# In the last three weight pieces of the mixing and dense stages, token tile 0 meets all three before tile 1 meets any

## The reference

```python
for layer in range(DEPTH):
    shift, scale, gate = ada_modulation(c, w_mod_mix[layer], b_mod_mix[layer])
    h = normalize(x) * (1.0 + scale) + shift
    mix = token_mixer(h, ...)          # projections, three branches, sigmoid gates, merged @ w_out
    x = layer_norm(DEEPNORM_ALPHA * x + (1.0 + gate) * mix, ln_mix_g[layer], ln_mix_b[layer])
    shift, scale, gate = ada_modulation(c, w_mod_ffn[layer], b_mod_ffn[layer])
    h = normalize(x) * (1.0 + scale) + shift
    ff = swiglu(h, ...) if layer % 2 == 0 else moe_swiglu(h, ...)   # dense 2816, or top 2 of 8 experts of 3584
    x = layer_norm(DEEPNORM_ALPHA * x + (1.0 + gate) * ff, ln_ffn_g[layer], ln_ffn_b[layer])
```

## Time and profile before

| | |
|---|---|
| median of 3 runs | 1868.97 us (1868.19 to 1871.65) |
| the profiled execution | 1872.58 us |
| its span in the trace | 1870.8 us |
| TensorE busy | 1721.1 us (92%) |
| VectorE busy | 1422.7 us (76%) |
| ScalarE busy | 1043.2 us (56%) |
| moved by DMA | 502.33 MB, 269 GB/s in the mean |

### The profile page before, as it was taken

One profiled execution on the slowest core, in us unless ns is written; L12 is line 12 of the kernel. 1 busy time (PEld: TensorE's weight loads), 2 busy tenths in 40 slices (PEclk: granted clock), 3 DMA queues, 4 the chain that ended last, 5 costly groups with the idle time before them and its releaser, 6 DMA issues.

```text
span 1870.8 us, 21981 instructions
## 1 busy us (share of the span) xinstructions
PE 1721.1 (92%) x7882; PEld 1380.4 (74%) x7883; DVE 1422.7 (76%) x1201; ACT 1043.2 (56%) x817; POOL 25.6 (1%) x31
## 2 busy tenths in 40 slices
PE   1899979997999958998999989999999999999995
PEld 0787758886877737876878878888788787787884
DVE  7776877766776785886888875556588788888887
ACT  1465434433455335765767755545477676776773
POOL 0100000000100000000000000000000000000000
PEclk9898989999999978999999999999999999999998
DMA  9874458765674345996998975676599899899991
GB/s 364 314 272 157 156 181 305 279 225 180 230 244 158 116 177 179 364 361 251 365 354 310 367 279 176 210 230 214 178 369 370 291 369 369 291 367 343 340 365 69
DMA packets 210536, 502.33 MB, mean 269 GB/s; under 512 B 9137, under 2 KB 13409, under 8 KB 210481
## 3 DMA queue, kind: packets, MB, share of 16 engines
q1 hardware_dynamic: 208770, 496.15, 74.7%
q0 software_dynamic: 1712, 5.43, 1.0%
HBM read 500.50 MB, written 1.05 MB: 268 GB/s over the span
## 4 chain that ended last, share of the span: by engine, by line
PE 84%; DVE 10%; issue 3%; ACT 1%; DMA 1%; POOL 0%; DVEq 0%; SPq 0%; ACTq 0%; POOLq 0%
PE ps L1343 24%; PE ps L1344 23%; PE ps L1345 23%; PE ps L1349 2%; PE ps L1350 2%; PE ps L1737 2%; PE ps L1850 2%; DVE mod_acc L853 1%; DVE w_lo L828 1%; PE ps L1778 1%; DVE stats L873 1%; PE ps L1467 1%; DVE gates L1022 1%; DVE hbuf L904 1%; DVE hbuf L907 1%
## 5 line engine op out<-in xcount | busy, mean ns | idle before, releaser
L1224 DVE TENSOR_TENSOR w_lo<-w_raw,w_hi 128x2048 fp32r<-128x2048 f32 x333 | 762.3, 2291 | 227.6 <-ACT w_hi L716 219.8
L716 ACT CAST w_hi<-w_raw 128x2048 fp32r<-128x2048 f32 x333 | 635.7, 1911 | 245.3 <-PE ps L1345 181.1
L1343 PE MATMUL ps<-w_hi,actT_hi 128*128 128x512 f32 (+1 forms) x1536 | 609.6, 397 | 22.5 <-issue 12.6
L1345 PE MATMUL ps<-w_hi,actT_lo 128*128 128x512 f32 (+1 forms) x1536 | 596.6, 388 | 0.0
L1344 PE MATMUL ps<-w_lo,actT_hi 128*128 128x512 f32 (+1 forms) x1536 | 596.2, 388 | 0.0
L1343 PEld LDWEIGHTS ps<-w_hi,actT_hi 128*128 128x128 f32 x1536 | 291.7, 190 | 88.2 <-issue 27.7
L1345 PEld LDWEIGHTS ps<-w_hi,actT_lo 128*128 128x128 f32 x1536 | 291.2, 190 | 60.5
L1344 PEld LDWEIGHTS ps<-w_lo,actT_hi 128*128 128x128 f32 x1536 | 292.0, 190 | 58.5 <-issue 2.4
L828 DVE TENSOR_TENSOR w_lo<-w_raw,w_hi 128x2048 fp32r<-128x2048 f32 x90 | 205.9, 2290 | 117.8 <-ACT w_hi L464 117.6
L464 ACT CAST w_hi<-w_raw 128x2048 fp32r<-128x2048 f32 x90 | 171.4, 1909 | 128.8 <-PE ps L1345 120.1
L1343 PE MATMUL ps<-w_hi,gT_hi 128*128 128x512 f32 x536 | 218.0, 407 | 17.0 <-DVE gT_lo L1247 13.1
(11 more groups left out here) (234 smaller groups left out, 1136.9 us busy)
## 6 DMA issues: line engine op xcount, KB each, us to landing
w_raw<-in_exp_w_dram SPq DMA_DIRECT2D x336, 1024.0 KB, 6.7
w_raw<-in_ffn_w_dram SPq DMA_DIRECT2D x33, 1024.0 KB, 5.3
w_raw<-in_w_mod_mix_dram SPq DMA_DIRECT2D x24, 1024.0 KB, 9.3
w_raw<-in_w_mod_ffn_dram SPq DMA_DIRECT2D x24, 1024.0 KB, 5.6
w_raw<-in_w_gate_dram SPq DMA_DIRECT2D x24, 1024.0 KB, 5.6
w_raw<-in_w_in_dram SPq DMA_DIRECT2D x14, 1024.0 KB, 7.1
w_raw<-in_w_out_dram SPq DMA_DIRECT2D x8, 1024.0 KB, 5.1
w_raw<-in_w_branch_c_dram SPq DMA_DIRECT2D x4, 1024.0 KB, 5.0
```

The source lines that it names most:

```text
L716: nc.scalar.copy(w_hi[:, i % SPLIT, :], w_raw[:, i % RING, :]).then_inc(split_hi, 1)
L1224: TTn(w_lo[:, i % SPLIT, :], w_raw[:, i % RING, :], w_hi[:, i % SPLIT, :].bitcast(F32), ALU.subtract).then_inc(piece_used, 1)
L1343: MM(to, hi, w_h, start=first, stop=False)
L1345: return MM(to, lo, w_h, start=False, stop=last)
```

## The change

Mixing: piece (1,0) runs on tile 0 alone, (0,1) waits for the merged half and runs on tile 0, (1,1) runs on tile 0 and signals `out_sent`; then tile 1 meets the three in the same order, and `split_used` is counted for each of them there. Dense: the same with (C,4,0), (C,4,1), (C,5,0); `turn(5)` comes behind (C,4,0) on tile 0. Panel 4's gT is then still needed when panel 5's is written, so panel 5's goes to other buffers, `gT_end_hi` and `gT_end_lo`, in the place of `h_lo`, which is not in use then. The streams of ScalarE and VectorE keep their order.

```diff
--- before.py
+++ after.py
@@ -266,6 +266,12 @@
         posm = sb("posm", [P, TT, EXPERTS + 1], scope=ffn)
         wsel = sb("wsel", [P, TT, EXPERTS + 1], scope=ffn)
         ffn.close()
+
+        gT_end_hi, gT_end_lo = (h_lo[:, part, 0:BANK].rearrange("p (b c q) -> p b c q", b=2, q=P) for part in range(2))
+        assert 2 * DENSE_PANELS[-1] == BANK
+
+        def gT_parts(p, panels):
+            return (gT_end_hi, gT_end_lo) if p == len(panels) - 1 else (gT_hi, gT_lo)
 
         ps = ctx.enter_context(nc.psum_tensor("ps", [P, 8, BANK], F32))
 
@@ -648,7 +654,7 @@
                         act.wait_ge(gT_sent, panel0 + p + 1)
                         w = panels[p]
                         for b in range(blocks):
-                            ins = A(gT_hi[:, b, 0:w // P, :], ps[:, HW1 + 2 * b, 0:w].rearrange("p (c q) -> p c q", q=P), ACT.Copy)
+                            ins = A(gT_parts(p, panels)[0][:, b, 0:w // P, :], ps[:, HW1 + 2 * b, 0:w].rearrange("p (c q) -> p c q", q=P), ACT.Copy)
                         ins.then_inc(gT_hi_ready, 1)
 
                     def after(j):
@@ -1111,8 +1117,8 @@
                         dve.wait_ge(gT_hi_ready, panel0 + p + 1)
                         w = panels[p]
                         for b in range(blocks):
-                            ins = TTn(gT_lo[:, b, 0:w // P, :], ps[:, HW1 + 2 * b, 0:w].rearrange("p (c q) -> p c q", q=P),
-                                      gT_hi[:, b, 0:w // P, :].bitcast(F32), ALU.subtract)
+                            hi, lo = (part[:, b, 0:w // P, :] for part in gT_parts(p, panels))
+                            ins = TTn(lo, ps[:, HW1 + 2 * b, 0:w].rearrange("p (c q) -> p c q", q=P), hi.bitcast(F32), ALU.subtract)
                         ins.then_inc(gT_lo_ready, 1)
 
                     def after(j):
@@ -1594,30 +1600,26 @@
                                     if j == 22 and t == 1 and k == 5:
                                         merged_T(0)
                         ins.then_inc(split_used, 1)
-                    elif h == 0:
-                        if n == 0:
-                            pe.wait_ge(mT_hi_ready, layer * 2 + 1)
-                            pe.wait_ge(mT_lo_ready, layer * 2 + 1)
-                        if n == 0:
-                            pe.wait_ge(branch_read, layer * 6 + 4)
+                    elif (n, h) == (0, 0):
+                        pe.wait_ge(mT_hi_ready, layer * 2 + 1)
+                        pe.wait_ge(mT_lo_ready, layer * 2 + 1)
+                        pe.wait_ge(branch_read, layer * 6 + 4)
                         for t in range(TT):
                             ins = project_out(j, n, h, t)
                         ins.then_inc(split_used, 1)
+                        merged_T(1)
+                    elif (n, h) == (1, 0):
+                        project_out(j, n, h, 0)
+                    else:
+
                         if n == 0:
-                            merged_T(1)
-                    elif n == 0:
-                        continue
-                    else:
-
-                        pe.wait_ge(mT_hi_ready, layer * 2 + 2)
-                        pe.wait_ge(mT_lo_ready, layer * 2 + 2)
-                        for t in range(TT):
-                            for m in range(2):
-                                ins = project_out(j - 1 + m, m, h, t)
-                                if t == TT - 1:
-                                    ins.then_inc(split_used, 1)
-                            if t == 0:
-                                ins.then_inc(out_sent, 1)
+                            pe.wait_ge(mT_hi_ready, layer * 2 + 2)
+                            pe.wait_ge(mT_lo_ready, layer * 2 + 2)
+                        ins = project_out(j, n, h, 0)
+                        if n == 1:
+                            ins.then_inc(out_sent, 1)
+                            for m, (n, h) in enumerate([(1, 0), (0, 1), (1, 1)]):
+                                project_out(j - 2 + m, n, h, 1).then_inc(split_used, 1)
                     after(j)
                 open_sublayer(layer * 2 + 1, 0, 4)
 
@@ -1641,10 +1643,11 @@
 
                     def down(j, p, h, b):
 
+                        hi, lo = gT_parts(p, panels)
                         for c in range(2):
                             k = 2 * h + c
                             for n in range(2):
-                                ins = product(bank(2 * b + n), gT_hi[:, b, k, :], gT_lo[:, b, k, :], *split_piece(j, c, n * BANK, D),
+                                ins = product(bank(2 * b + n), hi[:, b, k, :], lo[:, b, k, :], *split_piece(j, c, n * BANK, D),
                                               p == 0 and k == 0, p == len(panels) - 1 and k == panels[p] // P - 1)
                         return ins
 
@@ -1682,15 +1685,14 @@
                             if h == 0:
                                 pe.wait_ge(gT_hi_ready, panel0 + p + 1)
                                 pe.wait_ge(gT_lo_ready, panel0 + p + 1)
-                            if j == stretch.n_split - 2:
-                                continue
-                            if j == stretch.n_split - 1:
-                                for b in range(blocks):
-                                    ins = down(j - 1, p - 1, 1, b)
-                                    if b == blocks - 1:
-                                        ins.then_inc(split_used, 1)
-                                    ins = down(j, p, h, b)
-                                    ins.then_inc(split_used if b == blocks - 1 else y_sent, 1)
+                            if j >= stretch.n_split - SPLIT:
+                                ins = down(j, p, h, 0)
+                                if j == stretch.n_split - SPLIT:
+                                    turn(p + 1)
+                                if j == stretch.n_split - 1:
+                                    ins.then_inc(y_sent, 1)
+                                    for m, (_, p, h) in enumerate(stretch.pieces[-SPLIT:]):
+                                        down(j - SPLIT + 1 + m, p, h, 1).then_inc(split_used, 1)
                                 continue
                             for b in range(blocks):
                                 ins = down(j, p, h, b)
```

## The result

The changed kernel takes 1879.39 us in the median of ten runs (1873.85 to 1888.23), the kernel before 1871.86 us in ten beside it (1866.49 to 1874.33). The ratio is 1.0048 with an interval of 1.0031 to 1.0064: slower by 0.31 to 0.64%, 7.5 us between the medians. The sum of the prediction was +7.3 us. The ten runs of the kernel before include the three shown ahead, whose median was 1868.97, and its profiled execution. Experiment 6 measures the changed kernel once more and finds a smaller step, 4.5 us between the medians (ratio 1.0033, 1.0012 to 1.0053).

What follows compares the result with a forecast made beforehand. The prediction took the kernel as matmul-bound, with VectorE's sequence setting three joins. Terms +4.2 + 2.6 + 0.5 = +7.3 us on a median of 1868.97 gave 1876.3 us, range 1871.5 to 1880.5.

Steps and rivals of the forecast that it cites:

- What bounds the joins: Three stage ends where TensorE waits for VectorE's modulated tile: VectorE's sequence fills them, so a later first residual carries through fully.
- Join 1, +4.2: After layer 0's mixing: slot a released at matmul 48, rounding to residual 4.15 us; residual 4.13 us later plus 0.1 for a wait.
- The allowance of 0.1 us for a satisfied wait: TensorE's new wait for the merged half's remainder, expected to be covered, was costed at 0.1 us.
- Join 2, +2.6: After the dense stage: 4.15 us from matmul 48 to residual, less the 1.63 us gT_lo stall, plus 0.1 us.
- Join 3, +0.5: After layer 1's mixing: the DMA already held ahead(0); slot a's release moves the rounding from 655.12 to 655.6.
- The gain (start moves with tile 0): Rival: residual starts when tile 0 completes, 2.7 us earlier after layer 0's mixing, 1.6 + 2.7 after dense; sum -7.0, 5%.
- The dearer rival: Uncovered merged-half wait (up to 1.6 us, both mixing joins) or clock back 12 matmuls later; +10 to +13 together, 11%.
- the profiled execution would become 1879.9: Whole kernel: adding the summed +7.3 us to the earlier profiled execution's 1872.58 us gives 1879.9 us.

Runs made afterwards that it cites:

- Experiment 1: Changed kernel with ahead(0) moved behind the first square root on ScalarE and tile 0's statistics on VectorE: 1865.17 us, 0.9967 of the kernel before.
- experiment 4: Kernel before with only the dense stage reordered, slot a released before tile 0's end, and second gT buffers: 1868.05 us, 0.9983 of the kernel before.
- experiment 5: Changed kernel with ahead(0) moved in VectorE's order alone, ScalarE's order unchanged: 1867.81 us, ratio 0.9974 to the kernel before.

## Why the mechanism was right and one step of the time was not

- **What bounds the joins: right.** VectorE is busy for 29.59, 29.36 and 29.59 us of the 31 behind the first residual after the change, as before. A later start was carried in full; experiment 6's 176.3 us say the same of the stage behind.
- **Join 1, +4.2: measured 4.12 to 4.14.** Release of slot a at the 48th matmul, 4.15 us from rounding to residual, no visible stall at the merged half (VectorE's remainder of it ended at 231.35, b0 began at about 231.6). The allowance of 0.1 us for a satisfied wait was a little too much: the 49th matmul came 11.07 us behind the first, exactly as before. The satisfied wait at 234.33 shows as 0.28 us to the next start instead of 0.23.
- **Join 2, +2.6: measured 2.25.** Right in mechanism, too large by 0.35. The mis-sized term is the turn: I counted it as 0.6 us of TensorE's time, the duration in the earlier trace rows, but followed by matmuls it takes 0.35. The gain at the stall was therefore 1.87 us and not 1.63. The other 0.1 is again the allowance for a satisfied wait.
- **Join 3, +0.5: measured 0.40.** The DMA and the slot are late together, as said; the slot by 0.39 us more.
- **The rivals.** The gain (start moves with tile 0) is what the order would do if ahead(0) did not stand in front of it. Experiment 1 made it so and got it: the residual at c0's end. That its joins sum to 7.3 us less than before, close to the rival's 7.0, is chance: the rival had 2.7, 4.3 and 0, and the experiment has 0.52, 2.47 and 4.27, because ahead(0) is then paid inside each join and the DMA no longer holds join 3. The dearer rival did not come: neither the clock nor a stall at the new waits.
- **The step that failed: from the sum to a time.** Twice I added a right sum to a base that did not hold. The forecast of 1876.3 us is 7.3 above 1868.97, the median of three runs; ten runs of the same kernel give 1871.86. Against that base my time stands for a change of 4.4 us, a ratio of 1.0024, where 7.5 us (1.0048) were measured, 5.8 to 12 us by the interval. So the time names about half of the change, although the sum names all of it. The term that was off is the base, a median of three, 2.9 us below that of ten. The 3.1 us between 1876.3 and 1879.39 are 2.9 of base and 0.2 of sum. And "the profiled execution would become 1879.9" failed too: it became 1874.1, because the stretch of the experts was 7.2 us shorter in that trace, 5.4 of it in TensorE's waits. The prediction had taken all behind join 3 as equal, which two executions of one kernel need not be.
- **Where the sum was lucky.** 7.3 against 7.5 is closer than the evidence allows. The traces of the joins give 6.8, and the second set of runs of the changed kernel (experiment 6) gives 4.5 us, 2.2 to 9.9 by its interval. All agree with the sum, none to 0.2 us.
- **A size that was not forecast.** The stretch from the transposes of join 2 to piece a of join 3 took 1.5 us more (180.15 against 178.66). Over nine executions it is 177.4 to 180.2 us, and 180.15 and 178.76 for the changed kernel alone. The granted clock (fourth column) of its attention part differs with it, here before (178.66), after (180.15) and in experiment 4 (177.40):

```profile
545.50:592.00 46.50, 45.61 (x271) 0.86 0.53 186
```

```profile
552.70:599.20 46.50, 45.61 (x267) 0.84 0.53 180
```

```profile
543.60:590.10 46.50, 45.61 (x276) 0.89 0.54 187
```

## What to carry to other kernels

When the order of work on one engine is changed so that a result is ready sooner, ask what else that order released: here a buffer slot freed 12 matmuls after the result, where it had been freed 24 before it, held two in-order queues and turned 2.7 us of gain into 4.1 of loss. Work done ahead for the next stage may stand in front of the critical wait only while its buffer is free early enough (here 4.15 us ahead of it). Give a change as a difference or a ratio, and compare profiles by stretches between fixed points: the spans here differed by 1.5 us, the joins by 6.8.

## What the runs showed of the hardware

- A square root started 0.01 us after a table load of 1.28 us had ended, and the load 0.02 us after a rounding; no drain was seen (experiment 5, join 1).
- Four transposes in front of matmuls that need not wait took 0.35 us of TensorE's time, though their row says 0.60 (join 2).
- TensorE waited 2.5 to 5.9 us in all nine traces at the first matmul of the first expert, for nothing that the trace names, and in some executions another 3.4 to 5.0 us in a later expert (5.03 in the second one before, 4.13 in experiment 1). What it waited for is open.
- Idle times of TensorE from 8.8 to 13.5 us in join 1 left the stage behind at 176.27 to 176.31 us, so the length of the gap made no difference to what the clock cost after it.
